# Recurrence of a hybrid decoder step: chunk inverses in 32x32 blocks, transposes moved off TensorE, a new step order

## The chip, the cores and the metric

The kernel runs on one core of one Trainium2 chip. The metric is the device time of one execution in microseconds; the time before is the median of three runs, 2034.37 us. Engines are named as in the profile: PE is TensorE (PEld its weight loads), DVE VectorE, ACT ScalarE, POOL GpSimd, SP SyncE, whose queue issues the DMAs.

## The reference, cut to what matters

One inference step of a two-layer trunk: a prompt of 256 tokens and 8 sequences of 8 new tokens (320 columns together), model width 2048. Layer A is an RWKV-7 mixer, layer B stick-breaking attention over a paged cache. The change touches layer A's recurrence alone:

```python
def step(S, inp):
    r_t, w_t, k_t, v_t, kk_t, a_t = inp
    sa = jnp.einsum("bhvk,bhk->bhv", S, -kk_t)
    S = (S * w_t[:, :, None, :] + sa[..., None] * (kk_t * a_t)[:, :, None, :]
         + v_t[..., None] * k_t[:, :, None, :])
    o_t = jnp.einsum("bhvk,bhk->bhv", S, r_t)
    return S, o_t
...
o = ((o - mean) * lax.rsqrt(var + LNX_EPS) * lnx_g + lnx_b)
o = o + jnp.sum(r * k * r_k, axis=-1, keepdims=True) * v
o = o.reshape(B, T, D).astype(h.dtype) * jax.nn.silu(g)
```

There are 32 heads of 64 channels. r, k, v and g come from 2048x2048 projections, w (decay) and a from low-rank ones, kk is the normalised key.

## The kernel before, in words

Nearly all of the kernel is weight projections and the attention over the cache. Between the projection of g and that of the mixer's output (wo) lies the recurrence. It is computed in chunks of 64 tokens (`L`): the prompt is four chunks (`NCH`), the 64 sample tokens are a fifth (`CH` = 5), in which the eight sequences are 8x8 blocks. A tile is 128 channels, two heads; there are 16 tiles, and each two-head operand lies with head 0 on partitions 0 to 63 and head 1 on 64 to 127, so a matmul per head and chunk uses a 64x64 part of the array.

A tile goes through three stages, each in a slot of its own:
- **F (front)**: running sum of the log decay (`cs`), its exponentials (`Pc`, `Pi`, `Pm`), the normalised key (`sq`, `ss`, `ssm`, `ln`, `rn`, `kk`), and the scaled operands `Az`, `Rz` (in `AR`), `Bz`, `Kz`.
- **P (products)**: `AB` multiplies them for the four prompt chunks, `s4` for the sample. Masked, they give `D` (strictly lower, within 8x8 blocks), `FR`, `KK` and `S3`. Then the inverse of one minus the chunk's lower triangle is built: `D2`, `D4t`, `W`, `Y` are powers and partial products within 8x8 blocks, and `Yt`, `E`, `Et`, `E2`, `E2t`, `E4t`, `Z1`, `Z2`, `X` extend them over the 64x64 chunk. A name with t is a transpose, which TensorE makes by a matmul with the identity `I2`, as also `Vn`, `Bn`, `Kn`, the token-major forms of v, B and K. All results go to one of four PSUM banks and are copied out by ScalarE or VectorE (`READ_BY` says by which step; `free_p` waits for it).
- **R (run)**: per chunk c, `U`, `SA`, `S` and the state `ST`, each a small matmul and a small copy that wait for each other; outputs `O`; the sample's `Q4`, `U4`, `SA4`, `O4`, `SN`; then the group norm (`mean`, `cen`, `csq`, `var`, `lnv`, `rstd`, `on`, `ong`), `oy`, `y` and the split into `xh` and `xl` for the next projection.

In slot s, F works on tile s, P on tile s-1 and R on tile s-2. What stands in which order on an engine is set by one list, `ORDER`: an entry `P.t.AB` is stage, engine (t TensorE, v VectorE, a ScalarE, g GpSimd) and step. `AT` gives each entry its place as a fraction of the slot, `side_by_side` merges the stages' generators by it, and each engine then runs its part strictly in that order. Waits between steps are on counters per stage and engine (`Marks`). The SyncE queue has no generators: it issues the loads of a slot in the order s, k, r, a, v, the state `s0t`, the two stores and g, each behind waits for the steps that free its buffer. Slot 0 also holds the rest of g's projection, slot 17 the first of wo's.

Of the kernel before, what the change touches and what calls it, by code (L numbers as in the profile page):

```python
# [18 lines left out]
ALU = mybir.AluOpType  # L19
ACT = mybir.ActivationFunctionType  # L20

P = 128
# [7 lines left out]
L = 64  # L30
NCH = SEQ // L
# [297 lines left out]
F.a.sq F.a.ka1 R.t.U0 R.a.Q4 R.a.SA4 R.t.Q4 R.a.O0 P.t.AB R.t.SA0 R.g.Vnx R.v.U0 F.v.cs R.t.U4 P.t.s4 R.t.S0  # L329
F.a.kk0 R.v.SA0 R.t.SA4 R.a.SP1 R.t.O0 R.a.O4 F.t.ss R.t.U1 R.v.U4 P.a.Dt R.t.O4 P.t.Dt R.t.SA1 P.v.D R.t.SN  # L330
F.a.Pc P.a.D2t R.a.SP2 R.v.ST0 P.v.D4s P.a.D2 P.a.D4t R.t.S1 P.t.D2t P.t.D2 R.g.SAx F.a.ln F.g.k2 R.t.U2
R.a.O2 P.v.FR R.a.O1 F.a.rn F.a.Pi P.t.W R.t.SA2 R.a.O3 R.v.U1 P.v.KK F.a.Pm R.v.SA1 P.t.D4t R.t.S2 R.t.O2
P.v.s3 R.v.SNa R.v.ST1 F.g.csm R.v.U2 F.v.ssm R.a.SP3 R.v.SA2 P.g.ID P.a.Yt P.a.Vn R.t.O1 R.a.csq P.v.W
P.a.Et P.a.E R.t.U3 R.v.ST2 R.v.U3 P.t.Y R.t.SA3 P.t.Vn R.t.O3 R.a.lnv R.a.rstd P.t.Yt R.t.mean P.a.E2t
F.t.bon P.t.Et P.t.E R.v.SA3 P.v.Y R.t.var F.g.Rz F.g.ka P.t.Z1 P.a.E2 P.t.E2t F.v.rk R.v.cen F.v.kk P.t.E2
F.v.Az R.a.ong P.a.Bn P.a.E4t R.a.xh P.t.Bn F.v.Bz F.v.bonus P.v.Z1 P.t.Z2 P.t.E4t R.v.on P.v.Z2 P.t.Kn
R.t.S3 R.v.ST3 P.a.Kn F.g.Kz P.v.X P.t.X R.g.SNb R.g.oy R.g.y R.v.xl""".split()
# [50 lines left out]
def products_of_chunk(c_, pe, q, m, k, half=None, banks=None):  # L388
# [11 lines left out]
READ_BY = {"AB": ("v", "D", "FR", "KK"), "s4": ("v", "D4s", "s3"), "Vn": ("a", "Vn"), "Bn": ("a", "Bn"),  # L400
# [50 lines left out]
def make_masks(c_, pool):

    masks, blk, blkm, I2, m8, mFI, mSI, m3, keep, mJ = (
        c_.masks, c_.blk, c_.blkm, c_.I2, c_.m8, c_.mFI, c_.mSI, c_.m3, c_.keep, c_.mJ)
# [31 lines left out]
    for m in (m8, mFI, mSI, m3):  # L486
        made(pool.memset(m[:], 1.0))
# [8 lines left out]
    made(pool.tensor_copy(mFI[:, 1], mSI[:, 1]))  # L496
    made(pool.tensor_tensor(mFI[:, 0], mSI[:, 0], m8[:], ALU.subtract))
# [455 lines left out]
def recurrence(nc, c_, a):  # L953

    with ExitStack() as ctx:
# [11 lines left out]
        ins = {x: sb("in_" + x, [P, TOK]) for x in ("s", "k", "a", "r", "g")}  # L967
        vin = [sb(f"in_v{j}", [P, TOK]) for j in range(2)]
# [50 lines left out]
        def _(sp):  # L1019
# [20 lines left out]

            for x in ("k", "s", "a", "r", "v"):
                load(x, 0)
            load("g", 0)
            store_gate(2)
            for slot in range(TILES + 2):
                t, r = slot, slot - 2
# [6 lines left out]
                if t + 1 < TILES:  # L1053
                    F.v.wait(sp, "cs", t)
                    F.g.wait(sp, "csm", t)
                    load("s", t + 1)
                    F.a.wait(sp, "kk0", t)
                    F.a.wait(sp, "sq", t)
                    F.g.wait(sp, "k2", t)
                    load("k", t + 1)  # L1060
                    F.g.wait(sp, "Rz", t)
                    F.v.wait(sp, "rk", t)
                    load("r", t + 1)
                    F.a.wait(sp, "ka1", t)
                    F.g.wait(sp, "ka", t)
                    load("a", t + 1)
                    if t >= 1:
                        F.v.wait(sp, "bonus", t - 1)
                        Q.t.wait(sp, "Vn", t - 1)
                    load("v", t + 1)  # L1070
                if 0 <= t - 1 < TILES:

                    if t >= 3:
                        R.t.wait(sp, "Q4", t - 3)
                        R.v.wait(sp, "SNa", t - 3)
                    sp.dma_start(s0t[(t - 1) % 2][:], a["s0T"][t - 1]).then_inc(s0_in[(t - 1) % 2], 16)
                if 0 <= r < TILES:
                    R.v.wait(sp, "ST3", r)
                    sp.dma_start(a["o_wkv_p"][r], ST[3][:]).then_inc(wkvp_stored, 16)
                    R.g.wait(sp, "SNb", r)  # L1080
                    sp.dma_start(a["o_wkv_s"][r], SN[:]).then_inc(wkv_stored, 16)
                    if r + 1 < TILES:
                        R.g.wait(sp, "y", r)
                        load("g", r + 1)
# [6 lines left out]
        def _(pool):  # L1091
            pool.wait_ge(masks, c_.n_masks)

            def front(t):
                for name in steps_of("F", "g"):
# [1754 lines left out]
```

## Time and profile before

| | |
|---|---|
| median of 3 runs | 2034.37 us (2025.7 to 2036.75) |
| the profiled execution, own time | 2030.11 us |
| its span | 2028.4 us |
| mean granted TensorE clock | 0.982 of 2.4 GHz |
| busy share PE / DVE / ACT / POOL | 93% / 50% / 40% / 12% |

A row of a timeline gives the start and the time from the first record's start to the last one's end, engine, line, operation, output and inputs, tile rows*columns of the array, operand size, and the number of merged records. A float32 matmul leaves two records. An idle time in square brackets is that of the engine before the row, with what ended it.

### The profile page before, as it was taken

Reading aid. Unit: us, or ns where it says so; the run is one execution under the profiler, and the core shown is the slowest. Engines: PE = TensorE matmul, PEld = TensorE weight load, DVE = VectorE, ACT = ScalarE, POOL = GpSimd, SP = SyncE. Lnnn points to the kernel's source line nnn. Section 1 sums busy time; section 2 is a strip of 40 time slices with the busy share of each in tenths; the row PEclk is TensorE's granted clock in tenths of the full one; section 3 lists DMA queues with packets and bytes.
Section 4 is the critical chain, followed back from the end, with each engine's and each line's share of the span. In section 5 each row is a group of like instructions: output and inputs, shape, how many; then the busy total and the mean of one; then the engine's idle time right before and its main releaser. Section 6 shows DMA issues by size and latency. Waiting matters only on the chain.

```text
span 2028.4 us, 49604 instructions
## 1 busy us (share of the span) xinstructions
PE 1886.5 (93%) x20798; PEld 1623.7 (80%) x20798; DVE 1014.0 (50%) x1686; ACT 815.6 (40%) x1443; POOL 244.3 (12%) x308
## 2 busy tenths in 40 slices
PE   7999999999999999999999899999999999777797
PEld 7988999999888888879998677677777677343697
DVE  7744363634455556634544543443455444677344
ACT  4234232334455555523333333332333444655233
POOL 0200000000244444413200000000000000110032
PEclk9999999999999999989999999999999999999899
DMA  7545555544132322105488999999999999999541
GB/s 284 173 143 177 165 181 171 170 158 149 56 106 85 91 89 84 55 22 189 150 333 315 411 414 419 397 425 424 425 424 424 407 422 383 415 407 378 230 145 73
DMA packets 122959, 505.55 MB, mean 249 GB/s; under 512 B 16033, under 2 KB 55330, under 8 KB 77474
## 3 DMA queue, kind: packets, MB, share of 16 engines
q1 hardware_dynamic: 122754, 502.60, 64.9%
q8 instruction: 155, 2.54, 0.5%
q14 instruction: 50, 0.41, 0.1%
HBM read 470.24 MB, written 32.32 MB: 248 GB/s over the span
## 4 chain that ended last, share of the span: by engine, by line
PE 31%; DMA 16%; DVE 3%; ACT 2%; issue 2%; SPq 1%; DVEq 0%; ACTq 0%
DMA at_vraw<-in_cache_v 16%; PE psP L2566 8%; PE psP L2568 7%; PE psP L2567 7%; PE at_psO L2616 5%; PE at_psS L2595 3%; SPq L1979 1%; PE psP L2661 0%; PE at_psT L2607 0%; DVE wlo L2328 0%; SPq L2019 0%; DVE at_o_new L2483 0%; ACT at_p_w L2286 0%; ACT at_p_w L2284 0%; SPq L1997 0%
## 5 line engine op out<-in xcount | busy, mean ns | idle before, releaser
L2566 PE MATMUL psP<-xhi,whi 128*128 128x320 f32 x1488 | 477.6, 321 | 2.5 <-DVE xlo L2453 1.9
L2567 PE MATMUL psP<-xlo,whi 128*128 128x320 f32 x1488 | 462.3, 311 | 0.0
L2568 PE MATMUL psP<-xhi,wlo 128*128 128x320 f32 x1488 | 462.2, 311 | 0.0
L2566 PEld LDWEIGHTS psP<-xhi,whi 128*128 128x128 f32 x1488 | 282.0, 189 | 67.1 <-issue 66.4
L2328 DVE TENSOR_TENSOR wlo<-wraw,whi 128x2048 fp32r<-128x2048 f32 x92 | 212.9, 2315 | 209.0 <-ACT whi L2154 208.7
L2154 ACT ACTIVATE whi<-wraw 128x2048 fp32r<-128x2048 f32 x92 | 176.0, 1913 | 279.9 <-PE psP L2568 278.3
L2567 PEld LDWEIGHTS psP<-xlo,whi 128*128 128x128 f32 x1488 | 282.3, 190 | 0.1
L2568 PEld LDWEIGHTS psP<-xhi,wlo 128*128 128x128 f32 x1488 | 281.8, 189 | 0.0
L131 PE MATMUL psP<-xhi,whi 128*128 128x320 f32 x704 | 218.4, 310 | 2.8 <-DVE wlo L166 2.3
L132 PE MATMUL psP<-xlo,whi 128*128 128x320 f32 x704 | 217.8, 309 | 0.0
L133 PE MATMUL psP<-xhi,wlo 128*128 128x320 f32 x704 | 217.8, 309 | 0.0
L2616 PE MATMUL at_psO<-at_vraw,at_st 128*32 128x512 f32 x1000 | 129.2, 636 | 54.9 <-DMA at_vraw<-in_cache_v 45.8
L166 DVE TENSOR_TENSOR wlo<-wraw,whi 128x2048 fp32r<-128x2048 f32 x47 | 107.8, 2293 | 144.7 <-ACT whi L160 144.7
L160 ACT ACTIVATE whi<-wraw 128x2048 fp32r<-128x2048 f32 x47 | 89.8, 1910 | 161.9 <-PE psP L133 161.9
L131 PEld LDWEIGHTS psP<-xhi,whi 128*128 128x128 f32 x704 | 132.2, 188 | 3.9 <-DVE wlo L166 2.9
L132 PEld LDWEIGHTS psP<-xlo,whi 128*128 128x128 f32 x704 | 132.2, 188 | 0.1
L133 PEld LDWEIGHTS psP<-xhi,wlo 128*128 128x128 f32 x704 | 132.2, 188 | 0.0
L2595 PE MATMUL at_psS<-at_kraw,at_qp 128*32 128x256 f32 x2048 | 124.9, 385 | 0.2 <-DMA at_kraw<-in_cache_k 0.2
L2616 PEld LDWEIGHTS at_psO<-at_vraw,at_st 128*32 128x32 f32 x1000 | 27.5, 112 | 109.0 <-DMA at_vraw<-in_cache_v 59.4
L2231 ACT ACTIVATE at_st<-at_psT 128x256 f32<-128x256 f32 x64 | 24.3, 380 | 203.3 <-PE at_psT L2607 203.3
L2595 PEld LDWEIGHTS at_psS<-at_kraw,at_qp 128*32 128x32 f32 x2048 | 60.9, 111 | 46.3 <-issue 13.2
L394 PE MATMUL psP<-xhi,whi 128*128 128x320 f32 x256 | 89.2, 348 | 1.3 <-DVE wlo L166 0.8
(378 smaller groups left out, 3212.9 us busy)
## 6 DMA issues: line engine op xcount, KB each, us to landing
wraw<-in_weights SPq DMA_DIRECT2D x160, 1024.0 KB, 6.1
at_kraw<-in_cache_k SPq DMA_DIRECT2D x96, 1024.0 KB, 11.1
at_vraw<-in_cache_v SPq DMA_DIRECT2D x94, 1024.0 KB, 11.1
at_kraw<-in_cache_k SPq DMA_DIRECT2D x64, 512.0 KB, 9.5
at_vraw<-in_cache_v SPq DMA_DIRECT2D x62, 512.0 KB, 10.6
rw_s0t<-in_s0T SPq DMA_DIRECT2D x16, 256.0 KB, 3.1
o_wkv_s<-rw_SN SPq DMA_DIRECT2D x16, 256.0 KB, 2.3
resT<-in_xT SPq DMA_DIRECT2D x8, 320.0 KB, 5.1
```

What stands on the lines that cost most here:

```text
L131: pe.matmul(out, wh, c_.xhi[:, kc, :], start=(kc == 0), stop=False)
L132: pe.matmul(out, wh, c_.xlo[:, kc, :], start=False, stop=False)
L133: last = pe.matmul(out, wl, c_.xhi[:, kc, :], start=False, stop=(kc == NM - 1))
L160: act.activation(c_.whi[:, q % 2], c_.wraw[:, q], ACT.Copy).then_inc(c_.whi_ready, 1)
L166: dve.tensor_tensor(c_.wlo[:, q % 2], c_.wraw[:, q], c_.whi[:, q % 2], ALU.subtract).then_inc(c_.wlo_ready, 1)
L2154: act.activation(whi[:, i % 2], wraw[:, q], ACT.Copy).then_inc(c_.whi_ready, 1)
L2328: dve.tensor_tensor(wlo[:, i % 2], wraw[:, q], whi[:, i % 2], ALU.subtract).then_inc(c_.wlo_ready, 1)
L2566: pe.matmul(out, wh, c_.xhi[:, kc, :], start=(kc == 0), stop=False)
L2567: pe.matmul(out, wh, c_.xlo[:, kc, :], start=False, stop=False)
L2568: last = pe.matmul(out, wl, c_.xhi[:, kc, :], start=False, stop=(kc == NM - 1))
L2595: last = pe.matmul(psS[32 * j:32 * j + 32, 0:BK].rearrange("p (t s) -> p t s", t=KB), qp[:, b % 2, j, 32 * i:32 * i + 32], keys, start=(i ...
L2616: last = pe.matmul(psO[32 * g:32 * g + 32, :], st[:, k % 2, pg, 32 * g:32 * g + 32], values_of(k, pg, g), start=(k % NBLK == 0 and pg == 0 ...
```

## The change

What it does, in five parts:
1. **Blocks of 32.** The strictly lower triangle A of a chunk is compacted: `CA` holds its two diagonal 32x32 blocks of each head one above the other, 32 columns wide, taken out of PSUM by ScalarE (`C0`, `C04`, scaled by `side`, a 0/1 vector per partition) and added by VectorE (`C1`, `C14`). Inverses are made of the four diagonal blocks alone (`by_fourths`, four 32x32 matmuls per chunk), with one squaring fewer (E2t, Z1, X; no E4t, no Z2). The corner between the two blocks follows from `A12`, `Ht` and `XB`, two products of eight 64x64 matmuls with 32 columns.
2. **Transposes.** `Dt`, `D2t`, `Yt`, `Et`, `X1t` and those of v, B and K (`Vn`, `Bt`, `Kt`) are VectorE transposes, which turn each 32x32 block in its place.
3. **Block moves.** v is loaded once more with its blocks in place (`load_blocks_of_v`, four DMAs). For B and K, ScalarE copies all blocks (`Bn`, `Kn`), and four DMAs each (`move_blocks`) put the off-diagonal ones where they belong; S0 and SN wait for `turned_in`.
4. **SyncE's queue** is now merged from generators by `AT`: each load stands at the place of the step that frees its buffer.
5. **`ORDER`** is another one.

```diff
-F.a.sq F.a.ka1 R.t.U0 R.a.Q4 R.a.SA4 R.t.Q4 R.a.O0 P.t.AB R.t.SA0 R.g.Vnx R.v.U0 F.v.cs R.t.U4 P.t.s4 R.t.S0
...
+R.t.Q4 R.t.U0 P.t.AB R.g.Vnx R.a.Q4 F.a.sq R.v.U0 F.v.cs R.t.SA0 R.t.U4 P.a.C0 R.v.SA0 P.t.s4 R.v.U4 P.v.C1 R.t.S0
...
+            def loads_a(t):
+                yield max(AT["F.a.ka1"], AT["F.g.ka"])
+                F.a.wait(sp, "ka1", t)
+                F.g.wait(sp, "ka", t)
+                load("a", t + 1)
...
+            def load_blocks_of_v(t):
+                for h in range(2):
+                    for a_ in range(2):
+                        q = L * h + HL * a_
+                        src = spilled("v", t)[L * h:L * h + L].rearrange("(b q) (c a s) -> q c b a s", b=2, a=2, s=HL)
+                        sp.dma_start(VS[q:q + HL], src[:, :, :, a_]).then_inc(vs_in, 16)
+
+            def move_blocks(x, turned):
+                for h in range(2):
+                    for a_ in range(2):
+                        q, o = L * h + HL * a_, L * h + HL * (1 - a_)
+                        sp.dma_start(x[q:q + HL, :, HL * (1 - a_):HL * (1 - a_) + HL],
+                                     turned[o:o + HL, :, a_]).then_inc(turned_in, 16)
...
+                    if name == "C0":
+                        Q.t.wait(act, "AB", t)
...
+                        Q.a.done(act.activation(CA[:, 0:NCH], a_part[:, :, 0:HL], ACT.Copy, scale=c_.side[:, 0:1]), name)
...
+                    if name == "C1":
+                        Q.a.wait(dve, "C0", t)
+                        Q.v.done(dve.scalar_tensor_tensor(out=CA[:, 0:NCH], in0=quads[:, ab, :, 0, HL:L], scalar=c_.side[:, 1:2],
+                                                          in1=CA[:, 0:NCH], op0=ALU.mult, op1=ALU.add), name)
...
+                    elif name == "Dt":
+                        Q.v.wait(dve, "D", t)
+                        Q.v.done(dve.transpose(flat(Dt[:]), flat(D[:])), name)
...
-                def each(out, lhs, rhs, n):
+                def by_fourths(out, lhs, rhs, n):
 
                     for c in range(n):
-                        for r in halves:
-                            last = pe.matmul(out[r, c * L:c * L + L], lhs[r, c], I2[r, :] if rhs is None else rhs[r, c],
-                                             start=True, stop=True)
+                        for r in fourths:
+                            last = pe.matmul(out[r, c * HL:c * HL + HL], lhs[r, c], rhs[r, c], start=True, stop=True)
+                    return last
+
+                def corner(out, lhs, rhs):
+
+                    for c in range(NCH):
+                        for r in halves:
+                            last = pe.matmul(out[r, c * HL:c * HL + HL], lhs[r, c], rhs[r, c], start=True, stop=True)
                     return last
...
-                    elif name == "Vn":
-                        loaded(pe, "v", t)
-                        Q.t.done(each(ps, chunks(vin[j]), None, CH), name)
...
-                        Q.a.wait(pe, "Dt", t)
-                        Q.t.done(each(ps, D, Dt, CH), name)
...
+                        Q.v.wait(pe, "Dt", t)
+                        Q.t.done(by_fourths(ps, Dt, D, CH), name)
...
+                            if c == 0:
+                                pe.wait_ge(turned_in, 128 * (t + 1))
```

TensorE from the end of one tile's products to the next tile's AB, before. L1499 is `each`, L1473 mean and var, L1618 the queries against the sample's state (Q4), L1517 AB.

```order
L1499 MATMUL psP<-rw_E,rw_Et 64x64 x8
L1499 MATMUL psP<-rw_I2,rw_BZ1 64x64 x10
L1499 MATMUL psP<-rw_W,rw_D2t 64x64 x8
L1499 MATMUL psP<-rw_D2t,rw_D2 64x64 x8
L1499 MATMUL psP<-rw_I2,rw_KZ1 64x64 x10
L1600 MATMUL rw_psR<-rw_Vn0,rw_Kn0 64x64 x2
L1600 MATMUL rw_psR<-rw_SA3,rw_Bn0 64x64 x2
L1499 MATMUL psP<-rw_Dt,rw_D4t 64x64 x8
L1600 MATMUL rw_psR<-rw_Vn1,rw_KK1 64x64 x2
L1618 MATMUL rw_psR<-rw_AR2,rw_s0t1 64x2x8 x16
L1517 MATMUL psP<-rw_AR0,rw_BZ0 64x128 x2
```

The same place of the changed kernel; L1652 is `by_fourths`, L1659 `corner`, L1626 var and the bonus, L1754 Q4.

```order
L1652 MATMUL psP<-rw_Et,rw_E 32x32 x16
L1652 MATMUL psP<-rw_Y,rw_Et 32x32 x16
L1736 MATMUL rw_psR<-rw_Vn1,rw_Kn1 64x64 x2
L1736 MATMUL rw_psR<-rw_SA3,rw_Bn1 64x64 x2
L1626 MATMUL rw_psR<-stage_a,rw_blkm 64x320 x2
L1652 MATMUL psP<-rw_Z,rw_E2t 32x32 x16
L1659 MATMUL psP<-rw_XDt,rw_A12 64x32 x8
L1626 MATMUL rw_psF<-rw_rk,rw_blk 64x320 x2
L1659 MATMUL psP<-rw_XD,rw_Ht 64x32 x8
L1754 MATMUL rw_psR<-rw_AR0,rw_s0t0 64x2x8 x16
L1736 MATMUL rw_psR<-rw_Vn0,rw_KK0 64x64 x2
L1676 MATMUL psP<-rw_AR1,rw_BZ1 64x128 x2
```

The identity products with BZ and KZ are gone, var (the 64x320 row) and the bonus stand among the tile's last products now, and XB is the last before Q4, U0 and AB.

VectorE in the middle of a slot, before: from ST1 to SA3 of the running chunks.

```order
L1407 TENSOR_TENSOR rw_SN<-rw_psR,rw_s0t0 128x512
L1400 SCALAR_TENSOR_TENSOR rw_ST1<-rw_psR,rw_PC2,rw_SPr 128x64
L1389 COPY rw_U<-rw_psR 128x64
L1317 TENSOR_SCALAR rw_rn<-rw_psF 128x320
L1389 COPY rw_SA2<-rw_psR 128x64
L1378 TENSOR_TENSOR rw_W<-psP,rw_W 128x320
L1400 SCALAR_TENSOR_TENSOR rw_ST2<-rw_psR,rw_PC2,rw_SPr 128x64
```

And of the changed kernel, from ST1 to the sample's new state SN; the clamp `rn` is ssm.

```order
L1554 SCALAR_TENSOR_TENSOR rw_ST1<-rw_psR,rw_PC0,rw_SPr 128x64
L1513 STREAM_TRANSPOSE rw_D2t<-rw_D2 128x160
L1543 COPY rw_U<-rw_psR 128x64
L1506 TENSOR_TENSOR rw_S31<-psP,rw_m3 128x192
L1543 COPY rw_SA2<-rw_psR 128x64
L1533 TENSOR_TENSOR rw_W<-psP,rw_W 128x160
L1427 TENSOR_SCALAR rw_rn<-rw_psF 128x320
L1495 STREAM_TRANSPOSE rw_KT<-rw_KZ1 128x320
L1554 SCALAR_TENSOR_TENSOR rw_ST2<-rw_psR,rw_PC0,rw_SPr 128x64
L1561 TENSOR_TENSOR rw_SN<-rw_psR,rw_s0t0 128x512
```

SN's step moved from before ST1 to behind ST2, and the clamp and K's transpose stand between SA2 and ST2.

SyncE in one slot of the changed kernel; L1030 are the whole loads, L1043 the block moves, L1037 v's blocks, L1107 the state, L1112 and L1117 the stores. Before there were the same loads and stores without L1037 and L1043, in the order s, k, r, a, v, state, stores, g.

```order
L1107 DMA rw_s0t0<-in_s0T 128x512
L1030 DMA rw_in_k<-spill_k 128x320
L1030 DMA rw_in_s<-spill_s 128x320
L1043 DMA rw_Kn0<-rw_KT 32x5x32 x4
L1117 DMA o_wkv_s<-rw_SN 128x512
L1030 DMA rw_in_r<-spill_r 128x320
L1043 DMA rw_Bn0<-rw_BT 32x5x32 x4
L1037 DMA rw_VS<-spill_v 32x10x32 x4
L1030 DMA rw_in_a<-spill_a 128x320
L1112 DMA o_wkv_p<-rw_ST3 128x64
L1030 DMA rw_in_v<-spill_v 128x320
L1030 DMA rw_in_g<-spill_g 128x320
```

The state comes first and a near the end, with twelve block DMAs between.

## Rows read from the trace of the kernel before

**Rows 1.** The page's first part: busy us, share, instructions by engine.
```profile
PE 1886.5 (93%) x20798; PEld 1623.7 (80%) x20798; DVE 1014.0 (50%) x1686; ACT 815.6 (40%) x1443; POOL 244.3 (12%) x308
```

**Rows 2.** Line 1517 (AB): duration min/median/max in ns, first and last start.
```profile
L1517 PE MATMUL psP<-rw_AR,rw_BZ x256: 268/270/321, 522.9 to 856.0; 64*64 64x128 f32 x128
```

**Rows 3.** Windows, the stage's fifteen slots: busy by engine, PEclk, DMA share, GB/s.
```profile
522.90:854.40 331.50, 313.69 (x8414) 287.49 (x8416) 191.30 (x493) 188.50 (x531) 138.50 (x161) 1.00 0.28 83
```

**Rows 4.** Timeline of TensorE's matmuls in one slot.
```profile
704.05 0.31 PE L1600 MATMUL rw_psR<-rw_U,rw_X 64*64 64x64 f32 x4
704.29 0.66 PE L1649 MATMUL rw_psR<-rw_Vnx,rw_Kn 32*64 32x256 f32 x8
...
705.32 0.33 PE L1600 MATMUL rw_psR<-rw_Vn,rw_Kn 64*64 64x64 f32 x4
705.48 0.28 PE L1600 MATMUL rw_psR<-rw_SA,rw_Bn 64*64 64x64 f32 x4
705.60 0.75 PE L1499 MATMUL psP<-rw_Dt,rw_D 64*64 64x64 f32 x20
706.18 0.75 PE L1499 MATMUL psP<-rw_D,rw_Dt 64*64 64x64 f32 x20
...
713.06 0.66 PE L1499 MATMUL psP<-rw_Yt,rw_FR 64*64 64x64 f32 x16
713.52 0.66 PE L1499 MATMUL psP<-rw_FR,rw_Yt 64*64 64x64 f32 x16
...
720.46 1.11 PE L1618 MATMUL rw_psR<-rw_AR,rw_s0t 64*64 64x16 f32 x32 [0.31 <-ACT xhi L1262]
721.39 0.44 PE L1517 MATMUL psP<-rw_AR,rw_BZ 64*64 64x128 f32 x4
721.63 0.41 PE L1517 MATMUL psP<-rw_AR,rw_KZ 64*64 64x128 f32 x4
```

**Rows 5.** Timeline of VectorE in the same slot.
```profile
699.64 0.22 DVE L1389 COPY rw_U<-rw_psR 128x64 f32<-128x64 f32 x1
...
710.62 0.23 DVE L1389 COPY rw_SA<-rw_psR 128x64 f32<-128x64 f32 x1 [0.52 <-PE rw_psR L1600]
...
712.75 0.49 DVE L1412 TENSOR_TENSOR stage_a<-stage_a,rw_psR 128x320 f32<-128x320 f32 x1 [1.05 <-PE rw_psR L1473]
...
720.44 0.49 DVE L1418 TENSOR_TENSOR xlo<-rw_yv,xhi 128x320 fp32r<-128x320 f32 x1
720.85 0.22 DVE L1389 COPY rw_U<-rw_psR 128x64 f32<-128x64 f32 x1
```

**Rows 6.** Timeline of TensorE in the attention, 32-column tiles.
```profile
1751.23 0.65 PE L2650 MATMUL psP<-at_kN,at_qn 128*32 128x64 f32 x32
1751.81 0.38 PE L2682 MATMUL psP<-at_p_k,at_p_q 128*128 128x128 f32 x1
```

**Rows 7.** Groups by line and shape, VectorE, 535 to 875: busy us, mean ns.
```profile
L1341 DVE TENSOR_TENSOR rw_BZ<-rw_ka,rw_pi 128x320 f32<-128x320 f32 x15 | 17.0, 1136 | 11.3 <-POOL rw_ka L1122 11.3
L1389 DVE COPY rw_U<-rw_psR 128x64 f32<-128x64 f32 x75 | 16.7, 223 | 29.3 <-PE rw_psR L1600 28.2
...
L1378 DVE TENSOR_TENSOR rw_W<-psP,rw_W 128x320 f32<-128x320 f32 x15 | 7.2, 481 | 0.0
```

**Rows 8.** Line 1081, a DMA issue of SyncE, and its landing.
```profile
L1081 SPq DMA_DIRECT2D o_wkv_s<-rw_SN x16: 423/426/1621, 561.8 to 909.9; - x16
...
DMA to landing us min/median/max: 2.1/2.3/4.4
```

**Rows 9.** Windows, the slot after the last products, and one in the attention.
```profile
876.00:878.00 2.00, 0.71 (x8) 0.64 (x7) 1.14 (x3) 0.79 (x2) 0.97 (x2) 1.00 0.45 151
...
886.00:890.00 4.00, 4.00 (x33) 3.04 (x33) 0.23 (x1) 0.46 (x2) 0.00 (x0) 0.50 0.00 0
...
1139.80:1143.20 3.40, 3.40 (x16) 2.18 (x9) 3.40 (x5) 1.58 (x2) 0.00 (x0) 0.50 1.01 412
```

**Rows 10.** Waits in the fifteen slots: us in total, times, longest.
```profile
PEld psP L1499 <- issue: 7.4, 10, 1.5
```

More of the change, by code:

```diff
@@ L328 @@
 ORDER = """
-F.a.sq F.a.ka1 R.t.U0 R.a.Q4 R.a.SA4 R.t.Q4 R.a.O0 P.t.AB R.t.SA0 R.g.Vnx R.v.U0 F.v.cs R.t.U4 P.t.s4 R.t.S0
[L330 to L337, printed above, removed]
+R.t.Q4 R.t.U0 P.t.AB R.g.Vnx R.a.Q4 F.a.sq R.v.U0 F.v.cs R.t.SA0 R.t.U4 P.a.C0 R.v.SA0 P.t.s4 R.v.U4 P.v.C1 R.t.S0
+P.a.C04 R.t.SA4 F.a.kk0 F.t.ss P.v.C14 R.v.ST0 R.a.SA4 P.v.D F.a.Pc R.t.U1 P.v.Dt P.g.ID R.t.O4 R.v.U1 P.v.FR R.g.SAx
+R.t.SA1 R.a.O4 F.a.Pi P.t.D2 R.v.SA1 P.v.KK P.a.A12 P.g.F R.t.S1 R.a.SP1 P.a.D2 R.t.O1 R.v.ST1 F.a.ka1 R.t.O0 P.v.D2t
+R.t.U2 R.a.SP2 F.g.k2 R.a.O0 R.a.O1 P.t.W R.v.U2 P.v.s3 R.t.SA2 F.g.csm P.t.D4t R.v.SA2 P.v.W F.v.ssm R.t.S2 P.a.D4t
+R.t.SN F.g.Rz P.v.Kt F.a.ln R.v.ST2 F.a.Pm F.a.rn R.t.U3 R.v.SNa P.a.Kn P.t.Y R.v.U3 R.g.SNb P.v.Y R.t.SA3 R.t.O2
+R.v.SA3 P.v.Yt R.t.O3 P.v.Bt R.a.O2 F.v.rk P.t.E P.g.Y4 R.a.O3 R.t.mean P.a.E P.a.Bn P.v.Et R.v.cen P.t.E2t P.t.Z1
+P.v.Vn R.a.csq R.t.S3 F.v.kk P.a.E2t R.t.var P.v.Z1 F.g.ka P.t.X R.a.lnv F.g.Kz P.v.X R.a.rstd P.v.X1t P.a.Xa R.v.on
+P.t.Ht F.v.Bz R.a.ong F.t.bon P.a.Ht F.v.Az R.g.oy R.a.SP3 P.t.XB R.v.ST3 F.v.bonus P.a.XB R.g.y R.a.xh R.v.xl
+""".split()
 AT = {x: k / len(ORDER) for k, x in enumerate(ORDER)}
@@ new lines, in loads_blocks_of_v, with moves @@
+            def loads_blocks_of_v(t):
+                yield AT["P.v.Vn"]
+                Q.v.wait(sp, "Vn", t)
+                load_blocks_of_v(t + 1)
+            def moves(t):
+                for x in sorted("BK", key=lambda x: AT[f"P.a.{x}n"]):
+                    yield AT[f"P.a.{x}n"]
+                    Q.a.wait(sp, x + "n", t)
+                    if x == "B":
+                        move_blocks(Bn[t % 2], BT)
+                    else:
+                        move_blocks(Kn[t % 2], KT)
@@ L1041, in _, with loads_g @@
+            def loads_g(t):
+                yield AT["R.g.y"]
+                R.g.wait(sp, "y", t)
+                load("g", t + 1)
             for x in ("k", "s", "a", "r", "v"):
                 load(x, 0)
+            load_blocks_of_v(0)
             load("g", 0)
@@ L1052, in _ @@
                     load_weights(slot // 2 - 2)
[L1053 to L1084, printed above, removed]
+                none = iter(())
+                t, p, u = slot, slot - 1, slot - 2
+                ahead = t + 1 < TILES
+                side_by_side(states(p) if 0 <= p < TILES else none,
+                             loads_s(t) if ahead else none, loads_k(t) if ahead else none,
+                             loads_r(t) if ahead else none, loads_a(t) if ahead else none,
+                             loads_v(t) if ahead else none,
+                             loads_blocks_of_v(p) if 0 <= p < TILES - 1 else none,
+                             moves(p) if 0 <= p < TILES else none,
+                             stores_wkvp(u) if 0 <= u < TILES else none, stores_wkv(u) if 0 <= u < TILES else none,
+                             loads_g(u) if 0 <= u < TILES - 1 else none)
             for i in range(4, 7):
```

357 lines of the change are left out of this document (227 added, 130 removed), and 4 rows, old and new, of the table READ_BY.

## The prediction

> **What bounds the kernel now.** I read the page first, for the engines' shares: TensorE is busy 93% of the span, VectorE 50%, ScalarE 40% [rows 1]. The change touches one stage, the recurrence, so I cut that stage out. Its sixteen tiles follow each other in slots; the first product of a tile (AB, line 1517) starts at 522.9 us in the first tile, and its last record in the last tile at 856.0 [rows 2]. AB's eight groups of records start 0.24 apart at most [rows 4], so that record stands some 1.6 behind its tile's first, and fifteen slots take 331.5, **22.1 us each**. In that stretch TensorE is busy 313.7 of 331.5, VectorE 191.3 (12.8 a slot), ScalarE 188.5, GpSimd 138.5 (9.2), the granted clock is 1.00 (2.4 GHz) and the DMA engines carry 28% [rows 3]. TensorE is ahead, but "busy" counts matmuls to their modelled ends, so I looked at one slot in order of time.
>
> There the reader is to see the distance from one group's start to the next. Twenty records (ten matmuls of 64x64, each leaves two) go from 705.60 to 706.18: 0.58 us, 29 ns a record; sixteen go from 713.06 to 713.52: 0.47 [rows 4]. The queries against the sample's state, 32 records with 16 columns each, go from 720.46 to 721.39, the same 29 ns; four records of AB, 128 columns, take 0.24, twice as long each. VectorE tells the second story: the running state's chain goes from the first U copied (699.64) over SA3 (710.62) and the centred output (712.75) to xlo (720.44, 0.49 long), and the next U stands right behind it at 720.85 [rows 5]. From U to U that slot took 21.2, so 0.9 of the mean slot are stalls that this one was spared. Two things are thus nearly equally long: TensorE's list, and a chain R that goes through the whole slot in VectorE's fixed order.
>
> **The change, part by part.**
>
> *TensorE's products.* Removed per tile: nine groups of ten 64x64 matmuls and nine of eight (Vn, Bn, Kn, Dt, D2, D2t, W, D4t, Y; Yt, E, Et, E2, E2t, Z1, E4t, Z2, X): 9 x 0.58 + 9 x 0.47 = 9.45 us. Added: four groups of twenty 32x32 matmuls (D2, W, D4t, Y), four of sixteen (E, E2t, Z1, X), and Ht and XB, eight each with 64x64 weights and 32 columns. No row has 32x32. The nearest is line 2650, 32 records of 128*32 tiles with 64 columns in 1751.23 to 1751.81, less the change of shape at its end some 0.44: 13.9 ns a record [rows 6]. There four tiles run side by side, as the four diagonal blocks will, with twice the columns. Lower bound by columns: half of that, 6.9 ns; upper bound among rows: the 29 ns of the 16-column group. I take 6.9, because AB's rows scale with their columns [rows 4]: 4 x 0.27 + 4 x 0.22 = 2.0. Ht and XB load 64-row weights as the 16-column group does: 2 x 16 x 29 ns = 0.93. Sum 2.9.
>
> *Changes of tile shape.* Where a group of 32-row tiles follows one of 64x64 there is a hole: four records from 704.05 should end their turn at 704.17, the next group starts at 704.29; on the way back the group at 705.32 takes 0.16 in place of 0.12, and a part of the time before it [rows 4]. I take 0.15 us a change. The new order has seven places with 32x32 groups (D2, W, D4t, Y, E, E2t with Z1, X), fourteen changes: 2.1 us a slot. TensorE's list falls by 9.45 - 2.9 - 2.1 = **4.4 us**. The Trainium skill has this rule too (TensorEngine Tiling (Array Packing), Key Properties: changing the tiling mode drains the engine); the trace agrees, with 0.15 us. The same page (Instruction Overhead) says that a matmul with one column takes as long as one with sixty; that speaks against the change, since 32 columns would then bring nothing over 64. The 16-column group agrees with it, the 13.9 ns of rows 6 lie far under it; by that rule the sum would be the rival "floor" below.
>
> *VectorE.* Added per tile: eight transposes, three of 320 columns (Vn, Bt, Kt), two of 160 (Dt, D2t), three of 128 (Yt, Et, X1t), and C1, C14. No transpose is in the trace. Among its rows 320 columns take 481 ns from PSUM and 64 take 223 [rows 7], so 0.16 us and 1.0 ns a column: 3 x 0.48 + 2 x 0.32 + 3 x 0.29 + 0.65 for C1 and C14 = 3.6. Smaller operands give back (W, Y, Z1, X, D, FR; Z2 and D4s gone) about 1.6. VectorE goes from 12.8 to about 14.8 a slot. Upper bound for a 320-column operation: 1136 ns (BZ, which runs beside GpSimd) [rows 7].
> *ScalarE* loses thirteen copies and gets twelve, none with more columns. *GpSimd* gets F and Y4 and a shorter ID: level. Both at nothing; they have 9 and 13 us free in the slot [rows 3].
>
> *SyncE.* Twelve more DMA issues a slot (four blocks of V, four each of B and K) at 0.43 make 5 us more beside some 4 now, in 20: covered. Landing took 2.3 [rows 8]. B's blocks are issued after Bn (about 13.5 us into the slot) and are wanted by S0 of the next, about 9 us later; 4 x 0.43 + 2.3 = 4.0: hidden, with 5 us of slack. Small pieces of 128 bytes are not in the trace; twice the landing is still hidden. Behind Bn's wait on the queue stand V's blocks, a, the state, v and g, each wanted a good part of a slot later. That a is loaded after ka and used at the slot's first places now, and in its middle afterwards, only helps.
>
> *The slot that comes out.* TensorE alone would give 22.1 - 4.4 = 17.7. But chain R does not shrink by that. Worked out in the new order, AB's start as zero: one chunk (U copied 0.22, 0.14 to TensorE, SA 0.31, copy 0.22, 0.14, S 0.44, ST 0.28, 0.14, U 0.43) is 2.4, three make 7.3, and the last SA 1.0. Between U0 and SA0 stands AB (+1.9, less what U0's copy hides), before ST0 C14 and its ScalarE partner (+0.7), before ST1 KK (+0.2), before ST2 W, the clamp and Kt (+0.7), before U3 SN with two changes of shape, and SNa (+0.6): SA3 is copied at 11.9, 11.2 after U0's copy began, as it is today [rows 5]. O3, E and mean: centred at 13.9. The tail (squares, var, logarithm and exponential, scale, two GpSimd steps, xhi, xlo) is 7.1 when nothing is in its way (8.2 now, 712.75 to 720.93): xlo ends at 21.0, and the next U0 may be copied up to the end of the next AB: 21.0 + 0.4 - 1.9 = 19.5. The other closing chain is in TensorE's order: var issued at 15.1, X behind it, X added and transposed (Ht at 17.0), bon, XB only when ScalarE has Ht, which stands behind ong (18.65), the 16-column group 0.93, U0, and the next AB at **20.1**. I add half of today's stalls (0.45) and take 20.6: **1.5 us less in each of 16 slots, 24 us**. Against the profiled execution's own time, 2030.1 (span 2028.4), that is 2006; the median of the three runs is 4.3 higher, so **2010**. The case's own range is slots of 19.4 to 21.6: 1991 to 2026.
>
> **The rivals.**
> *The clock falls (0.20).* Today's list keeps the array streaming; the new one leaves holes at the slot's end (X, Ht, XB, 16-column group). The rows show what that can do: after TensorE sat idle most of 876 to 878 and then ran the 16-column group, the granted clock stood at 0.5 (1.2 GHz) from 886 to 890 though the engine was busy all the time [rows 9]. Elsewhere it stood there for 3.4 us (1139.8 to 1143.2). At most half of such a stretch is lost: 1.7 x 16 = 27, the whole gain: 2037. It decides against the change from 14 slots of 16 on; in half of them it leaves 2023. Against it: holes of up to 1.5 us in today's slots [rows 10] left the clock at 1.00 [rows 3].
> *VectorE becomes the bound (0.13).* With transposes at twice my price VectorE has 17.7 busy, and five of them (Dt, D2t, Kt, Yt, X1t) stand in one of the two chains: 4 x 0.3 + 0.5 = 1.7 more a slot, 22.3: 2037. From 1.5 on the gain is gone. BZ's 1136 ns speaks for it, the 481 against.
> *Floor per matmul (0.05), the one that ends slower.* If 32x32 records cost 29 ns whatever their columns, 288 records take 8.4, with Ht and XB and the changes 11.4 against 9.45: slot 24.1, 2.0 x 16 = 32: 2066. From 22 ns a record on TensorE's list is no shorter than now. Rows 6 speak against it.
> *The block moves come late (0.07).* If B's blocks land over 9 us after Bn, S0 waits; 2 us late costs 32: 2042. It would show as a DMA wait before S0.
>
> **How the numbers follow.** My forecast has 0.55. The range that leaves out 2 in 10 goes from 1988 (slot 19.2) to 2045 (the clock rival with a little more, the late moves). A measurement of this kernel tells 0.5%, 10 us, from no change. Faster: 0.93 of the forecast, a fifth of the clock rival, parts of the others: 0.60. Within 0.5%: 0.22. Slower: 0.18.
>
> **What would show it.** AB to AB 20.6; 40 records of a 32x32 group in 0.27 to 0.3 us; holes of 0.15 at each change of shape; VectorE's 320-column transpose near 0.48; TensorE's busy share in the stage down to about 80%; the granted clock at 1.00. Wrong if the clock is under 0.95 there, if transposes are near 1 us, or if ST0 to ST2 wait for VectorE's own queue longer than worked out.

## The result and the profile after

The changed kernel takes 2060.69 us (median of 4 runs, 2057.55 to 2065.42), the kernel before 2032.57 in the same comparison: ratio 1.0144, 95% interval 1.0108 to 1.0179. It is slower by some 28 us, where I had forecast 2010. Every ratio below is to the kernel before, run in the same comparison; its median lay between 2027.2 and 2032.6 in the five of them, so a difference between two variants is good to some 5 us. Its profiled execution (own time 2060.8) has a span of 2059.1 against 2028.4, and a mean granted clock of 0.951 against 0.982.

The page's first part of the changed kernel:

```profile
span 2059.1 us, 49829 instructions
PE 1877.8 (91%) x20734; PEld 1575.4 (77%) x20734; DVE 1027.2 (50%) x1814; ACT 794.6 (39%) x1427; POOL 250.7 (12%) x357
```

Shares hardly move from [rows 1], so I went by stretches: the fifteen slots from the first AB to the last, and a stretch behind them (columns as in [rows 3]).

```profile
522.44:876.02 353.58, 298.71 (x8356) 238.23 (x8358) 201.86 (x612) 168.29 (x517) 136.09 (x191) 0.86 0.36 92
893.40:927.50 34.10, 32.13 (x285) 23.86 (x289) 5.07 (x17) 4.89 (x15) 2.90 (x4) 0.50 0.04 9
```

Against 331.5 us in [rows 2, 3] the slots take 353.58, **23.6 us each** in place of 22.1 (and of my 20.6). That is 22.1 of the 30.7 us. The first AB starts 0.5 earlier; 9.1 us come behind the last AB. The hundredth record of wo's products stands 67.9 us behind it (59.3 before), and ahead of that the granted clock is at 0.50 (1.2 GHz) for 34 us (13.7 before). In the slots it is 0.86: in all 99 of 354 us at half clock, none before. TensorE is less busy than before (298.7 against 313.7), in more time. The view of waits, TensorE's own rows of that stretch (time in all, times, longest):

```profile
PE psP L1652 <- issue: 23.4, 18, 3.2
PE psP L1659 <- DVE rw_XDt L1522: 9.3, 10, 0.9
PE psP L1659 <- ACT rw_X L1321: 4.5, 5, 0.9
PE rw_psR L1736 <- issue: 3.7, 5, 1.3
```

L1652 is the group of 32x32 products. With three rows under 1 us, TensorE waited 28.6 us for "issue", nothing that the profile names. Before, the same rows sum to 10.3:

```profile
PE psP L1499 <- issue: 6.0, 8, 1.4
PE rw_psR L1618 <- issue: 2.8, 6, 0.8
PE rw_psR L1600 <- issue: 1.5, 6, 0.4
```

I had seen such holes and used them only as evidence on the clock. One of them in order of time:

```profile
640.11 0.31 PE L1736 MATMUL rw_psR<-rw_ST,rw_AR 64*64 64x64 f32 x4
640.39 0.44 PE L1652 MATMUL psP<-rw_W,rw_D2t 32*32 32x32 f32 x29
644.01 0.31 PE L1652 MATMUL psP<-rw_W,rw_D2t 32*32 32x32 f32 x11 [3.18 <-issue]
644.25 0.33 PE L1736 MATMUL rw_psR<-rw_U,rw_X 64*64 64x64 f32 x4
```

It stands **inside** a group: 29 records run, 11 come 3.2 us later, with every operand there since the group began. No wait on another engine's data can do that. DMA traffic in the stretch before the hole and in it, by queue:

```profile
q1 hardware_dynamic: 99, 0.36, 90.6%
...
q1 hardware_dynamic: 374, 0.50, 68.3%
q8 instruction: 1, 0.02, 2.4%
```

The first row is 640.70 to 641.70 (no packet of instructions), the others 641.70 to 644.01: the one 16 KB packet that was wanted starts at 641.73, and TensorE goes on 2.3 us later. All 24 holes over 0.35 us that stand at a record without a wait of its own (28 us) end 2.2 to 2.9 us behind the start of such a packet, though packets are 4.9 us apart in the median; so do the eleven of the kernel before. The hole shown is the extreme one: its packet starts 0.9 us after TensorE has stopped. In the other 23 it is on its way for 0.7 to 2.5 us when the hole opens, and TensorE runs out before it can be used. From 534 to 876 us queue 8 brings 66 packets for 16,130 records of loads and products, one for 244:

```profile
q8 instruction: 66, 1.08, 1.3%
```

The Trainium skill (Runtime: NRT & Kernel Launch, Instruction fetch mechanics) says that a sequencer fetches its instructions in blocks of 16 KiB, 256 instructions, and that this is mostly hidden. Size and count agree with the trace; "hidden" does not, with 28.6 us here.

The number of instructions in all is not what grew. The changed kernel has 16,714 such records in its fifteen slots, the one before 16,830, so a little fewer for each us (47 against 51). What is new is how densely some of them stand.

The clock around the hole (columns as above):

```profile
637.70:641.10 3.40, 3.07 (x128) 2.66 (x123) 2.61 (x9) 2.31 (x10) 2.35 (x5) 1.00 0.96 344
641.10:644.30 3.20, 0.29 (x13) 0.25 (x13) 0.00 (x0) 0.00 (x0) 1.56 (x2) 1.00 0.69 232
644.30:647.70 3.40, 3.40 (x69) 2.06 (x68) 1.56 (x5) 1.83 (x5) 0.00 (x0) 0.53 0.02 5
```

TensorE idles at 1.00 and then works at 0.53 (nearly all of it 1.2 GHz). The DMA engines are 96% busy ahead of the hole: SyncE had issued a 1 MB load of weights at 636.84. So there were four suspects: the supply of instructions, the clock, that load, and the small pieces of the block moves.

### The profile page after: what moved, and what is told of

Read it like the earlier page. It is cut to its first block, busy times and chain, and to the rows that moved or that the text cites. A ratio compares the mean times of both kernels' runs of the same rounds, so it can differ in the third digit from the quotient of the medians.

```text
span 2059.1 us, 49829 instructions
## 1 busy us (share of the span) xinstructions
PE 1877.8 (91%) x20734; PEld 1575.4 (77%) x20734; DVE 1027.2 (50%) x1814; ACT 794.6 (39%) x1427; POOL 250.7 (12%) x357
## 4 chain that ended last, share of the span: by engine, by line
PE 30%; DMA 17%; DVE 3%; issue 2%; ACT 2%; SPq 1%; DVEq 0%; ACTq 0%
DMA at_vraw<-in_cache_v 17%; PE psP L2700 7%; PE psP L2702 7%; PE psP L2701 7%; PE at_psO L2750 5%; PE at_psS L2729 3%; SPq L2113 1%; PE psP L2795 0%; PE at_psT L2741 0%; DVE at_o_new L2617 0%; ACT at_p_w L2420 0%; DVE at_p_rc L2645 0%; ACT at_p_w L2418 0%; SPq L2153 0%; DVE at_w L2550 0%
## 5 line engine op out<-in xcount | busy, mean ns | idle before, releaser
L2729 PE MATMUL at_psS<-at_kraw,at_qp 128*32 128x256 f32 x2048 | 129.4, 395 | 0.0
L2365 ACT ACTIVATE at_st<-at_psT 128x256 f32<-128x256 f32 x64 | 24.4, 381 | 203.7 <-PE at_psT L2741 203.7
```

Source lines behind the costliest of these rows:

```text
L2729: last = pe.matmul(psS[32 * j:32 * j + 32, 0:BK].rearrange("p (t s) -> p t s", t=KB), qp[:, b % 2, j, 32 * i:32 * i + 32], keys, start=(i ...
```

## The experiments

Theory S (supply): the 32x32 groups use instructions up faster than they come. Theory C: the clock. "Slot" is the mean from AB to AB over fifteen slots, "issue" the sum of TensorE's issue rows there, "half" the time there at 0.5.

**One matmul for all chunks.** In the function of the 32x32 groups:

```
-    for c in range(n):
-        for r in fourths:
-            last = pe.matmul(out[r, c * HL:c * HL + HL], lhs[r, c], rhs[r, c], ...)
+    for r in fourths:
+        last = pe.matmul(out[r, 0:n * HL], lhs[r, 0], flat(rhs[r, 0:n]), ...)
```

> The changed kernel, but each group of 32x32 products is issued as four matmuls over all chunks' columns, with the first chunk's weights, in place of sixteen or twenty: the result is no inverse any more, the columns are the same, and of 288 records a tile 64 are left. Theory S (supply): the groups of 32x32 take TensorE's instructions faster than they are brought in; the changed kernel shows 28.6 us in which TensorE waited for nothing but issue in its fifteen slots, 10.3 before. Then this falls to 8 or less, a slot from 23.6 to 22 or less, and the time by 20 to 30 us, to 2030 to 2040. Theory C (clock): the holes at the slot's end and the few columns bring the granted clock down to half in 99 us of 354, and that is the cost; columns and holes are as before, so the clock stays near 0.86 in the stage and the time within 8 us of 2060.

Measured: 2005.43, ratio to before 0.9901 (0.9868 to 0.9934).

```profile
523.55:824.87 301.32, 270.60 (x4997) 194.41 (x4999) 200.73 (x612) 167.95 (x517) 135.94 (x191) 0.92 0.41 107
PE psP L1651 <- issue: 2.1, 2, 1.2
q8 instruction: 42, 0.69, 1.0%
```

Same columns, VectorE's work and block moves; 55 us less. It is not the groups' own time: at full clock D2's group takes 0.48 us from its start to that of the next one, in forty records and in eight alike. Issue 28.6 to 2.7, slot 20.09. S holds, more strongly than I gave it; C's forecast (within 8 us) falls, though half clock went from 99 to 48 us with the holes.

**Pairs of chunks.** The same with `range(0, n, 2)` and 64 columns.

> As the merged run, but only pairs of chunks are taken together: a matmul has 64 columns with the first chunk's weights, 160 records of the 32x32 groups a tile in place of 288 (64 in the merged run); the result is no inverse. It gives the dose of theory S: if the cost goes with the number of records, 2025 to 2032, midway; if a stall comes only where a burst outruns the supply, under 2015, with 8 us or less of issue waits.

Measured: 2017.29, ratio 0.9945 (0.9922 to 0.9969); slot 20.83, issue 16.3, half 43. The time lies between the two forms that I had written: 288, 160 and 64 records give 23.6, 20.8 and 20.1 us a slot, so the first 128 taken away are worth 2.7 and the next 96 only 0.7: it bends as a threshold would. The issue waits do not: 16.3 are left, the longest of 3.4 and 3.7 us behind loads of 1 MB.

**Long products as a filler.** Ahead of the waits of X, Ht and XB, into the bank that they then write:

```
+    for _ in range({"X": 1, "Ht": 1, "XB": 1}.get(name, 0)):
+        over_channels(ps[:, 0:320], blk, keep[:, 0:320])
```

> The changed kernel with three extra products a tile, each of two 64x64 blocks by 320 columns (about 0.55 us), issued into the bank that X, Ht and XB are about to write, just ahead of their waits; nothing else. Theory C: the clock comes back to 0.97 or more in the stage, the slot falls from 23.6 to 22.5 or less, 2060 to 2045 or less. Theory S: the clock may rise, but the issue waits inside the 32x32 groups stay at 25 us or more, and the time stays within 6 us of 2060, or rises by what of the 1.6 us a slot is not covered.

Measured: 2051.67, ratio 1.0096 (1.0066 to 1.0126); clock 0.92, half 58, slot 23.39. Nine us less than the changed kernel by the medians (every run is under each of its runs), of which the profiled slots show 2.8, while issue rose to 35.8:

```profile
PE psP L1652 <- issue: 19.5, 21, 1.8
PE rw_psR L1738 <- issue: 14.7, 8, 4.8
```

More work on TensorE made the kernel faster, so the clock costs something; it is not the larger part. Both forecasts were too clean.

**The filler where supply is no matter.** Both edits together.

> The merged run (first chunk's weights for all, no inverse) with the three extra products a tile of the filler run. It prices the clock where the supply is no matter: the merged run had 48 us of 301 at half clock. Theory C: the clock in the stage goes from 0.92 to 0.98 or more and the slot from 20.1 to 19.6 or less, the time from 2005 to 1998 or less. If the low clock falls where TensorE has slack, nothing or a few us more: 2003 to 2012.

Measured: 1989.73, ratio 0.9808 (0.9765 to 0.9851).

```profile
522.38:815.75 293.37, 275.44 (x5177) 189.58 (x5179) 199.25 (x612) 169.32 (x517) 135.73 (x191) 0.99 0.42 110
```

Half clock 48 to 7 us, slot 20.09 to 19.56, thirteen of the fifteen between 19.6 and 20.0. So 41 us of half clock cost 8 us in the slots (16 by the medians). The Trainium skill (TensorE: Matmul & The Clock Gate, Terms) prices such time at half of itself, an estimate of 20 us; here the profile shows less, presumably since in part of it TensorE waits for the chain through VectorE anyway.

**The inverses alone.** The changed kernel with Vn, Bn and Kn again as TensorE's products (one group each behind D2, SA2 and O3), copied by ScalarE, without block moves or their three transposes.

> One part of the change alone: the compact 32x32 inverses, with values, B and K again turned by TensorE (three groups of ten 64x64 products between the 32x32 groups) and copied by ScalarE, no block moves. If the block moves and VectorE's transposes of 320 columns are the cost, it is at or under the kernel before, 2033 or less. Theory S: the stalls stay, somewhat fewer since 64x64 products stand between the groups: 2045 to 2060. Theory C: clock 0.90 to 0.95, 2045 to 2055, with little issue wait.

Measured: 2082.26, ratio 1.0280 (1.0246 to 1.0315), worse than both. Slot 24.91, issue 18.6, half 81. The stalls are there without block moves, fewer, as S has it, but the 30 products come on top. My order for them is not a planned one; how much is its fault stays open.

**Values, B and K alone.** The kernel before with VectorE's three transposes, the block moves and the new queue; Vn, Bn and Kn gone from TensorE. Kt stands behind s3, Bt behind W, Vn behind rk.

> The other part alone: the kernel before, its 64x64 inverses and its order, with values, B and K turned by VectorE and moved in blocks by DMA, and SyncE's queue in the order in which buffers come free. Theories S and C both expect a clock of 1.00 in the stage, issue waits of 10 us or less, and 2010 to 2032, since TensorE has 30 products fewer a tile. If the moves or the transposes are the cost, it is at 2045 or more, with waits for them.

Measured: 2045.77, ratio 1.0080 (1.0051 to 1.0109); both theories missed, and the time is that of the third case, moves or transposes as the cost.

```profile
522.06:867.19 345.13, 296.73 (x7516) 265.61 (x7517) 208.53 (x537) 186.10 (x516) 138.23 (x161) 0.99 0.35 93
PE rw_psR L1670 <- ACT rw_Q L1292: 11.7, 9, 2.3
PE psP L1578 <- DVE rw_W L1457: 11.2, 15, 0.8
ACT rw_k L1266 <- DMA rw_in_a<-spill_a: 18.8, 13, 4.6
```

Issue is low (7.6) and the clock at 0.99, yet the slot grew from 22.1 to 23.0. TensorE lost 1.7 us of products a slot and got waits. The first row, 11.7 us, is the load of a in the end, as the order of time shows:

```profile
656.15 0.54 SPq L1023 DMA_DIRECT2D rw_in_a<-spill_a  x1
660.35 0.65 ACT L1266 ACTIVATE rw_k<-rw_in_a,rw_less_ka,vec 128x320 f32<-128x320 f32 x1 [1.99 <-DMA rw_in_a<-spill_a]
660.91 0.25 ACT L1292 ACTIVATE rw_Q<-rw_psR 128x128 f32<-128x128 f32 x1
661.31 0.33 PE L1670 MATMUL rw_psR<-rw_Vn,rw_S 64*64 64x64 f32 x4 [1.59 <-ACT rw_Q L1292]
```

SyncE issues a behind the eight block moves, late for a step that stands at the start of the old order; ScalarE waits for it ahead of the copy of Q, and TensorE for that copy. It is so in all nine of these waits (ScalarE starts 0.02 us behind a's landing), and the kernel before has none for a. The second row is VectorE's W (2.5 us before), whose list is 1.1 a slot longer. The places are mine, so this shows that the shift can cost, not that it must, and its largest wait comes from the new queue under the old order, not from the transposes.

**Bursts in the kernel before, and their control.** Ahead of D2, Y and E2, into the bank that they then write: forty records of 32x32, or as control `over_channels(ps[:, 0:320], blk, keep[:, 0:320])`.

```
+    for c in range(CH):
+        for r in fourths:
+            pe.matmul(ps[r, 32 * c:32 * c + 32], I2[r, 0:32], keep[r, 0:32], ...)
```

> The kernel before with three extra groups of 40 records of 32x32 a tile, of no use, into the bank that D2, Y and E2 are about to write: by the changed kernel's rows 0.36 us each and 0.21 for the changes of shape, 1.7 us a slot; 240 instructions more a tile, no block moves, no transposes on VectorE. Theory S: bursts on top of a list with few holes outrun the supply, issue waits from 10.3 to 20 us or more in the fifteen slots, and the time 10 us or more over that of the control below. If bursts alone are harmless, issue waits stay at 12 or less and both runs agree within 5 us.

> Control of the run with bursts: the kernel before with three extra products of two 64x64 blocks by 320 columns a tile at the same places, 0.55 us each, 1.65 us a slot, with 24 instructions more a tile. Both theories: clock 1.00, issue waits 10 us or less, slot 22.1 to 23.7 (what part of the 1.65 us the chain through VectorE covers is seen here), time 2030 to 2056.

Measured: bursts 2071.85, ratio 1.0189 (1.0152 to 1.0226); control 2036.24, ratio 1.0055 (1.0037 to 1.0073). The waits and the stage, bursts first:

```profile
PE psP L1499 <- issue: 10.1, 18, 1.2
PE rw_psR L1605 <- issue: 7.1, 10, 1.1
524.90:891.54 366.64, 342.21 (x10216) 310.73 (x10217) 190.45 (x492) 191.12 (x530) 138.33 (x161) 1.00 0.25 76
...
PE psP L1499 <- issue: 1.9, 2, 1.1
522.65:858.95 336.30, 329.94 (x8597) 296.77 (x8597) 190.88 (x492) 189.31 (x530) 138.32 (x161) 1.00 0.27 82
```

Planned for nearly the same time on TensorE, 36 us apart (no run of one is among those of the other), at a clock of 1.00 in both, with no block moves and no transposes: 21.6 us of issue waits against 4.6, slots of 24.4 against 22.4 (the profiled executions are the slowest of the bursts and the fastest of the control, 45 us apart). Of the 30 us between the two stages 17 are issue waits, S by itself. 12 are TensorE's busy time (342.2 against 329.9), in part the changes of shape around the bursts. And the control says that 1.65 us more of TensorE's work a slot cost 0.3 (9 us in all by the medians): in the kernel before, TensorE's list had room and was **not** the only bound.

**Block moves doubled.** Each move of B and K a second time, into a tile that nobody reads.

> The changed kernel with each of the eight block moves of B and K issued twice a tile, the second time into a tile that nobody reads. If the small pieces of the block moves hold TensorE's instructions up or come late themselves, issue waits go from 28.6 to 35 or more, or waits of S0 for the moves show, and the time rises by 8 us or more. If not, within 5 us of 2060 (SyncE has 3.5 us more to issue a slot).

Measured: 2077.79, ratio 1.0248 (1.0218 to 1.0278); slot 24.65, half 112.

```profile
PE rw_psR L1738 <- issue: 19.3, 13, 3.1
PE psP L1654 <- issue: 18.8, 15, 3.0
```

Issue 28.6 to 39.3, but not by supply. Eight of the waits in the first row, 14.4 us, stand at S0, which waits for the moves' semaphore, as here:

```profile
567.91 0.60 SPq L1045 DMA_DIRECT2D rw_again<-rw_BT  x1
569.89 0.33 PE L1738 MATMUL rw_psR<-rw_Vn,rw_Kn 64*64 64x64 f32 x4 [2.77 <-issue]
```

The last move is issued 2.0 to 2.8 us ahead of the end of each of these waits, about the 1.9 to 2.3 us that a move takes to land in the changed kernel; the profile has no landing for the moves of this run, and so calls the wait "issue". Without them 24.9 us are left, no more than the 28.6. So the doubled moves cost by coming late, and no share of the changed kernel's holes is shown to be theirs: there they land 3.6 to 9.9 us ahead of S0.

**The loads in sixteen pieces.** The four loads of 1 MB cut into sixteen of 256 KB, two a slot, in the changed kernel and in the kernel before (the lines are of the latter):

```
-                elif slot in (4, 6, 8, 10):
-                    load_weights(slot // 2 - 2)
+                if 4 <= slot < 12:
+                    load_piece(2 * (slot - 4))
...
+                if 4 <= slot < 12:
+                    load_piece(2 * (slot - 4) + 1)
```

> The changed kernel with the four loads of 1 MB of the next matrix's weights cut into sixteen of 256 KB, two in each of eight slots, and nothing else. The longest waits of TensorE for issue (3 to 4 us each, in this kernel, in the pairs and in the shared run) stand 2 to 4 us behind such a load's issue, and the packet of instructions that ends them starts late. If the loads hold the instructions up: those waits are 1.5 us at most, issue waits in all 28.6 down to 22 or less, time 2060 down to 2048 to 2055. If the bursts of 32x32 records alone make the waits, all stays within 4 us of 2060.

> The kernel before with its four loads of 1 MB cut into sixteen of 256 KB, nothing else. Its issue waits are 10.3 us in the fifteen slots, 1.5 and 1.3 of them behind such loads: a gain of 2 to 5 us at most, 2024 to 2030, that is no change that can be told.

Measured: 2066.18, ratio 1.0172 (1.0133 to 1.0210), and 2048.84, ratio 1.0087 (1.0063 to 1.0112). The longest wait fell from 3.2 to 2.2 us, but there are more of them and the sum is 30.0; the theory of the loads falls as an account of the total. In the kernel before the pieces even cost 18 us: the state's load stands behind a piece in SyncE's queue (landing 4.1 us where it was 3.1), TensorE's products that follow it wait 9.9 us in nine slots, each until 0.09 us behind its landing, and half clock appears there too, 27 us.

**Fewer instructions for the same result.** W and D4 use the same weights (D2t), so do Z1 and E2 (Et): one group with 64 columns each, W beside D2 and Y beside E in one tile. VectorE turns D4 and E2 straight from PSUM; ScalarE's two copies go.

```
+    def by_fourths_of_two(out, lhs, rhs, n):
+        out = out[:, 0:2 * n * HL].rearrange("p (x c l) -> p x c l", x=2, l=HL)
+        for c in range(n):
+            for r in fourths:
+                last = pe.matmul(out[r, :, c], lhs[r, c], rhs[r, :, c], ...)
```

> The changed kernel with the same result from fewer instructions: W's and D4's products share their weights and run as one group with 64 columns (so do Z1's and E2's), VectorE transposes D4 and E2 straight from PSUM in place of ScalarE's copies; 216 records of 32x32 groups a tile in place of 288, two transposes more on VectorE (0.65 us a slot). Theory S: issue waits from 28.6 to 12 to 20 us, slot from 23.6 to 22.3 to 23.0, time 2035 to 2050. If VectorE's chain is what binds, as when values, B and K alone were moved to it, the slot stays at 23.3 or more and the time at 2055 or more.

> The shared weights and the three extra products of the filler run together. If supply and clock each cost a part of their own: 9 us under the shared run, 2026 to 2041, about the kernel before (2030). If the clock falls only because of the stalls, no more than 4 us under the shared run.

> Shared weights, three extra products a tile, and the loads cut into sixteen: the sum of what was found. The shared run with the filler (2020.6) had slots of 22.0, 22.5 and 25.3 behind three of the loads where the slots beside them had 19.9 to 20.5: 9 us. Theory: 2010 to 2016, slot 20.3 to 20.7, a version faster than both kernels. If the loads do not matter: 2017 to 2024.

> The fastest version (shared weights, three extra products, loads in sixteen pieces) with a fourth extra product ahead of Z1's wait, where TensorE waits 0.5 us for E's transpose. Half clock was 24 us of 316 there. If the clock still costs: 2012 to 2016. If what is left is stalls: 2015 to 2021.

Measured: shared 2039.34, ratio 1.0063 (1.0040 to 1.0087), slot 21.98, issue 16.2, half 63; with the filler 2020.58, ratio 0.9972 (0.9947 to 0.9998), slot 21.01, issue 10.6, half 24; with the loads in pieces as well 2017.65, ratio 0.9927 (0.9903 to 0.9951), slot 21.05; with a fourth filler 2018.69, ratio 0.9945 (0.9925 to 0.9965), slot 21.38. Shared weights came as forecast: 21 us by a quarter fewer 32x32 records. The filler on top gave 19 more, 5 better than forecast and more than its 9 alone; issue waits fell too, by 5.6, so not all of it is the clock. The loads in pieces and the fourth filler bring nothing that can be told. The third is faster than both kernels, by 13 us against the kernel before.

```profile
521.79:836.95 315.16, 284.17 (x7457) 215.16 (x7459) 205.95 (x642) 162.32 (x487) 135.86 (x191) 0.96 0.39 103
```

## Why the prediction was wrong, step by step

**The step that failed: TensorE's list as a sum of durations.** I took 20 or 16 matmuls of 32x32 to cost their own time wherever they stand. Their own time was nearly right, and the instructions are what does not keep up: the 128 to 160 loads and products of two such groups leave in under a microsecond, and the next packet, which brings some 244, is of use only 2.2 to 2.9 us after it starts. With that cost taken away (one matmul for all chunks) the slot is 20.1, with the clock up 19.6: against 23.6, supply and what it drags along are 3.5 us a slot, the rest of the clock 0.5. Of these 3.5, 1.7 are issue waits themselves; the rest goes with 51 us less of half clock. My row for it was in front of me: [rows 10] show holes of up to 1.5 us with the releaser "issue" in a group of the kernel before. I asked only whether they let the clock fall.

**The rivals.** The clock rival was real but sized from its end: it fell for 99 us in the slots, and where supply is no matter the 41 us that the filler takes back cost 8. It had no term for what makes the holes. "Floor per matmul" came nearest in time (2066) by another mechanism: no floor, 9 ns a record, but a rate of supply. VectorE as the bound: not by the transposes' price. Late block moves: no wait of S0 for them shows in the changed kernel (they land 3.6 us ahead at least); with the moves doubled it does, 14.4 us.

**Durations.** Forty records of 32x32 go from the first to the last in 0.36 us (0.27 to 0.30 expected), 32 in 0.26 (0.22); the step into such a group is 0.15 where it is 0.03 otherwise, out of it 0.12: 0.2 a pair of changes, 0.3 expected. With 0.9 for Ht and XB the products and changes that I added at 2.9 + 2.1 come to 3.4 + 1.5: the sum of durations is right to 0.1 us, and the slot is 3 us off. The transposes were right:

```profile
L1485 DVE STREAM_TRANSPOSE rw_Vn<-rw_VS 128x320 f32<-128x320 f32 x15 | 7.5, 503 | 0.0
L1510 DVE STREAM_TRANSPOSE rw_Dt<-rw_D 128x160 f32<-128x160 f32 x15 | 5.2, 346 | 0.5
L1516 DVE STREAM_TRANSPOSE rw_Yt<-rw_Y 128x128 f32<-128x128 f32 x15 | 4.5, 302 | 0.0
```

Forecast 480, 320 and 290 ns. VectorE has 13.5 us a slot (14.8 forecast), TensorE is busy 84% (80%).

**The chains.** With supply and clock out of the way the slot is 19.6 where I worked out 20.1 and 0.45 of stalls: right in kind, one us long. Of TensorE's tail one half is seen as I wrote it: ahead of Ht it waits 0.9 us in every slot for X's transpose (the rows of 9.3 and 4.5 us above; the second names ScalarE's copy of X, which ends at about the same time and which Ht does not read). XB's wait for ScalarE's Ht, which I had in the chain, does not show. What I had wrong of the kernel before is the weight of TensorE's list: the control with long products shows it had room.

**Of the 9 us behind the last AB**, the profile shows where 8.6 arise: by 944 us, with 20 us more at half clock ahead of that. Over all seventeen profiles the time behind the last AB (1170 to 1185 us) goes with the half clock in it (63 us in the shortest, 97 in the changed kernel with its 1183; correlation 0.78). That makes the clock the likely cause, but no run changed it alone there, so it stays open.

## What to carry to other kernels

Count instructions as well as time, and in the densest microseconds, not in sum: both kernels here have the same number a tile. Many small matmuls in a row are limited by how fast the instructions arrive, and a hole in the middle of a group, with the releaser "issue", is its mark. At a record that waits for a semaphore "issue" can also be a DMA whose landing the profile lacks, as with the doubled moves: look at what the instruction waits for. When small tiles save columns, put products with the same weights into one matmul before asking for smaller ones. A hole costs more than itself where the granted clock falls behind it, so a useless product in a wait can pay; test it rather than argue it.

## What the runs showed of the hardware that I had not expected

TensorE's instructions come as packets of 16 KB on a DMA queue of their own, one for 244 records. Holes end 2.2 to 2.9 us after a packet's start. The longest, 3.2 us here and 3.7 with pairs, end 7 to 9 us behind the issue of a load of 1 MB; that eight more small moves a slot make more of them is not shown. A 32x32 matmul with 32 columns costs 9 ns a record (0.36 us for 40), far under the 29 ns of a 64x64 one with 16 columns. Extra products on TensorE made a kernel faster in all three places where half clock was over 40 us (by 9, 16 and 19 us), and in the kernel before, which had none in the slots, slower by 0.55%.
